# Depthwise convolution of a two-layer decoder step: four channel blocks on VectorE, four on TensorE between the pointwise blocks

## The reference

```python
def conv_module(x, prev, g_norm, w_pw1, b_pw1, w_dw, b_dw, g_ln, b_ln, w_pw2, b_pw2):
    h = rms_norm(x, g_norm)
    u = h @ w_pw1 + b_pw1
    a, gt = jnp.split(u, 2, axis=-1)
    u = a * jax.nn.sigmoid(gt)
    full = jnp.concatenate([prev, u], axis=1)
    c = lax.conv_general_dilated(full, w_dw[:, None, :], window_strides=(1,), padding='VALID',
                                 dimension_numbers=('NWC', 'WIO', 'NWC'),
                                 feature_group_count=CONV_CH) + b_dw
    c = jax.nn.silu(layer_norm(c, g_ln, b_ln))
    return x + c @ w_pw2 + b_pw2, full[:, -(CONV_W - 1):]
```

## Time and profile before

| | us |
|---|---|
| median of 3 runs | 1651.44 (1649.75 to 1652.22) |
| the profiled execution | 1650.97, its span 1648.9 |
| TensorE matmul busy | 1539.7 (93% of the span) |
| VectorE busy | 1276.7 (77%) |
| ScalarE busy | 960.0 (58%) |
| GpSimd busy | 159.9 (10%) |
| the stretch of the convolution stage, from the first pointwise block to the last mean matmul | 20 to 161 |

### The profile page before, as it was taken

One profiled execution on the slowest core, in us unless ns is written; L12 is line 12 of the kernel. 1 busy time (PEld: TensorE's weight loads), 2 busy tenths in 40 slices (PEclk: granted clock), 3 DMA queues, 4 the chain that ended last, 5 costly groups with the idle time before them and its releaser, 6 DMA issues.

```text
span 1648.9 us, 22208 instructions
## 1 busy us (share of the span) xinstructions
PE 1539.7 (93%) x7880; PEld 1291.9 (78%) x7880; DVE 1276.7 (77%) x1285; ACT 960.0 (58%) x999; POOL 159.9 (10%) x135
## 2 busy tenths in 40 slices
PE   6776899999988879999999999999999999999998
PEld 5765799999966768877877887887887887887886
DVE  5999545455686447888888888888888888888886
ACT  5420544344554246676667677677667677667674
POOL 5661111011230010000000000000000000000000
PEclk9888899999987979999999999999999999999999
DMA  8731234544533138988898898998998998998992
GB/s 329 141 115 31 77 136 158 176 158 166 180 97 143 52 124 305 350 347 339 348 369 325 338 373 324 350 356 328 353 360 322 338 365 329 358 356 331 345 359 115
DMA packets 64322, 431.38 MB, mean 262 GB/s; under 512 B 7862, under 2 KB 10166, under 8 KB 13713
## 3 DMA queue, kind: packets, MB, share of 16 engines
q1 hardware_dynamic: 57312, 412.38, 66.0%
q0 software_dynamic: 3616, 12.28, 3.2%
q10 hardware_dynamic: 3344, 6.05, 1.1%
HBM read 422.55 MB, written 9.14 MB: 262 GB/s over the span
## 4 chain that ended last, share of the span: by engine, by line
PE 77%; DVE 13%; issue 4%; ACT 3%; DMA 1%; POOL 1%; ACTq 0%; DVEq 0%; POOLq 0%
PE bank L334 23%; PE bank L336 23%; PE bank L335 23%; DVE odd L1175 2%; DVE C L1175 2%; PE bank L720 2%; DVE w_lo L1120 2%; ACT w_hi L1014 2%; DVE w_lo L1396 1%; PE bank L356 1%; PE bank L590 1%; PE bank L702 1%; PE bank L703 1%; DVE oe_lo L1538 1%; DVE d_lo L1493 1%
## 5 line engine op out<-in xcount | busy, mean ns | idle before, releaser
L1396 DVE TENSOR_TENSOR w_lo<-land,w_hi 128x2048 fp32r<-128x2048 f32 x224 | 504.1, 2289 | 109.9 <-ACT w_hi L1014 108.9
L1014 ACT CAST w_hi<-land 128x2048 fp32r<-128x2048 f32 x224 | 417.4, 1910 | 3.5 <-issue 3.5
L334 PE MATMUL bank<-w_hi,xe_hi 128*128 128x512 f32 x896 | 365.8, 408 | 0.6 <-DVE xe_lo L1482 0.6
L335 PE MATMUL bank<-w_lo,xe_hi 128*128 128x512 f32 x896 | 355.3, 397 | 0.0
L336 PE MATMUL bank<-w_hi,xe_lo 128*128 128x512 f32 x896 | 354.8, 396 | 0.0
L1017 ACT CAST d_hi<-land 128x2048 fp32r<-128x2048 f32 x112 | 214.1, 1912 | 125.3 <-PE bank L336 125.3
L1493 DVE TENSOR_TENSOR d_lo<-land,d_hi 128x2048 fp32r<-128x2048 f32 x112 | 256.7, 2292 | 23.9 <-ACT d_hi L1017 16.0
L336 PEld LDWEIGHTS bank<-w_hi,xe_lo 128*128 128x128 f32 x896 | 168.8, 188 | 41.0
L334 PEld LDWEIGHTS bank<-w_hi,xe_hi 128*128 128x128 f32 x896 | 168.8, 188 | 34.9 <-issue 1.0
L335 PEld LDWEIGHTS bank<-w_lo,xe_hi 128*128 128x128 f32 x896 | 169.3, 189 | 33.2
L334 PE MATMUL bank<-d_hi,heT_hi 128*128 128x512 f32 x448 | 178.4, 398 | 5.5 <-DVE heT_lo L1515 5.5
(11 more groups left out here) (244 smaller groups left out, 2289.4 us busy)
## 6 DMA issues: line engine op xcount, KB each, us to landing
land<-in_w_expert SPq DMA_DIRECT2D x336, 1024.0 KB, 5.1
land<-in_w_dense SPq DMA_DIRECT2D x54, 1024.0 KB, 4.8
rel_rows<-rb POOLq DMA_DIRECT2D x1, 3072.0 KB, 37.9
bias<-rel_rows ACTq DMA_DIRECT2D x4, 512.0 KB, 5.9
X<-in_x SPq DMA_DIRECT2D x4, 288.0 KB, 5.9
out_y<-X SPq DMA_DIRECT2D x2, 576.0 KB, 2.8
Us<-in_state POOLq DMA_DIRECT2D x1, 1088.0 KB, 9.5
out_conv_s<-Us POOLq DMA_DIRECT2D x1, 1088.0 KB, 6.5
```

What stands on the lines that cost most here:

```text
L334: pe.matmul(out, w[0], x[0], start=start, stop=False)
L335: pe.matmul(out, w[0], x[1], start=False, stop=False)
L1014: act.copy(w_hi[n % RING][:], land[(DENSE + u) % LAND][:]).then_inc(hi_done, 1)
L1396: dve.tensor_tensor(w_lo[n % RING][:], land[slot][:], w_hi[n % RING][:].bitcast(F32), ALU.subtract).then_inc(split, 1)
```

## The change

VectorE takes the prompt convolution of channel blocks 0, 2, 4 and 6, TensorE that of 1, 3, 5 and 7. TensorE runs the first three of its four directly behind pointwise blocks 3, 5 and 7, the fourth behind the third. ScalarE writes the diagonals, one 128x128 activation for each tap (identity, scaled by the tap's weight), the next channel block's as TensorE leaves each group. ScalarE no longer scales taps. VectorE also makes the window products of the sample convolution. Its taps behind the pointwise blocks are now 9, 3, 3, 33, 3, 33 and 3. GpSimd has no arithmetic left between the first low parts of the activations and those of the second matrix; it only issues its DMAs, the rows of the relative bias as soon as they are there, the two states when all of `Up` is.

```diff
-PE_CONV = 3
-POOL_CONV = 1
-DVE_CONV = KT_D - PE_CONV
-TAPS_BETWEEN = 6
+DVE_CHANNELS = [0, 2, 4, 6]
+PE_CHANNELS = [1, 3, 5, 7]
+CONV_BEHIND = {3: 0, 5: 1, 7: 2}
+TAPS_BEHIND = [9, 3, 3, 33, 3, 33, 3]
...
+            def conv(m):
+                if m == 0:
+                    pe.wait_ge(rb_ready, 1)
+                if m >= 2:
+                    pe.wait_ge(cp_ready, m - 1)
+                pe.wait_ge(u_ready, PE_CHANNELS[m] + 1)
+                for g, taps in enumerate(GROUPS):
+                    pe.wait_ge(diag_ready, CW * m + taps[-1] + 1)
+                    for w in taps:
+                        last = pe.matmul(bank[4 + m % 2][:, 0:SEQ], diag[:, g, w - taps[0], :],
+                                         Up[:, PE_CHANNELS[m], w:w + SEQ], start=(w == 0), stop=(w == CW - 1))
+                    last.then_inc(diag_used, 1)
+                pe.wait_ge(diag_used, len(GROUPS) * (m + 1))
+                pe.sem_inc(cv_done, 1)
...
+                if j in CONV_BEHIND:
+                    conv(CONV_BEHIND[j])
+            conv(3)
...
-            by_end = [*range(DVE_CONV - 1), *range(DVE_CONV, KT_D), DVE_CONV - 1]
+            by_end = [0, 2, 1, 3, 4, 5, 6, 7]
...
+            def diagonals(m, g):
+
+                if m >= 1:
+                    act.wait_ge(diag_used, len(GROUPS) * (m - 1) + g + 1)
+                for w in GROUPS[g]:
+                    act.activation(diag[:, g, w - GROUPS[g][0], :], ident, ACT.Identity,
+                                   scale=w_dw[:, PE_CHANNELS[m], w:w + 1]).then_inc(diag_ready, 1)
+
+            def conv_out(m):
+
+                act.wait_ge(cv_done, m + 1)
+                act.activation(C[:, PE_CHANNELS[m], 0:SEQ], bank[4 + m % 2][:, 0:SEQ], ACT.Identity,
+                               bias=v("b_dw", PE_CHANNELS[m])).then_inc(cp_ready, 1)
...
-                for w in range(4 * j, min(4 * j + 4, CW)):
-                    tap(w)
+                if j < 2:
+                    diagonals(0, 2 * j)
+                    diagonals(0, 2 * j + 1)
+                if j in CONV_BEHIND:
+                    for g in range(len(GROUPS)):
+                        diagonals(CONV_BEHIND[j] + 1, g)
+                    conv_out(CONV_BEHIND[j])
...
-                dve.wait_ge(win_ready, j + 1)
+                first = Us[:, j, :, 0:1]
+                windows = bass.AP(tensor=first.tensor, offset=first.offset,
+                                  ap=[list(first.ap[0]), [DS + CW - 1, NB], [1, DS], [1, CW]])
+                dve.wait_ge(u_ready, j + 1)
+                seq(dve.tensor_tensor(win[:], windows, w_dw[:, j, :].unsqueeze(1).unsqueeze(1).to_broadcast(
+                    [P, NB, DS, CW]), ALU.mult))
...
-            taps = [(j, w) for j in range(POOL_CONV, DVE_CONV) for w in range(CW)]
+            taps = [(j, w) for j in DVE_CHANNELS for w in range(CW)]
...
-                if j >= POOL_CONV:
-                    for t in taps[TAPS_BETWEEN * (j - 1):TAPS_BETWEEN * j]:
+                if j < KT_D - 1:
+                    for t in taps[sum(TAPS_BEHIND[:j]):sum(TAPS_BEHIND[:j + 1])]:
                         tap(*t)
             sample_conv(KT_D - 1)
-            for t in taps[TAPS_BETWEEN * (KT_D - 1):]:
+            for t in taps[sum(TAPS_BEHIND):]:
                 tap(*t)
...
-            def diagonals(m):
...
-            def add_tap(w):
...
+            pool.wait_ge(rb_ready, 1)
+            per_head = P * RLEN
+            pool.dma_start(bass.AP(tensor=io["rel_rows"].tensor, offset=0,
+                                   ap=[[per_head, NH], [RLEN, P], [1, RLEN]]),
+                           rb[:].unsqueeze(1).to_broadcast([NH, P, RLEN])).then_inc(rb_stored, 16)
+            pool.wait_ge(u_ready, KT_D)
             pool.dma_start(io["conv_p"], Up[:, :, SEQ:SEQ + CW - 1]).then_inc(conv_stored, 16)
             pool.dma_start(io["conv_s"], Us[:]).then_inc(conv_stored, 16)
```

More of the change, by code:

```diff
@@ L133, in build @@
         g_q8 = sb("g_q8", [P, 1])
-        prod = raw[:, :, 0:SEQ]
         phases = [0]
@@ L214, in build @@
         diag_ready, diag_used, cv_done, cp_ready = (sem(n) for n in ("diag_ready", "diag_used", "cv_done", "cp_ready"))
[L215 to L218, removed]
+        in_dw, cs_ready = (sem(n) for n in ("in_dw", "cs_ready"))
+        c_ready, mean_ready, xc_ready, ln_ready = (
+            sem(n) for n in ("c_ready", "mean_ready", "xc_ready", "ln_ready"))
         pw2_done, x_conv = sem("pw2_done"), sem("x_conv")
@@ L377, in _ @@
                     pe.matmul(bank[5][0:NH, 0:RLEN], relb[:, :], buckets[:, :], start=True, stop=True).then_inc(rel_sum, 1)
[L380 to L393, removed]
+                if j in CONV_BEHIND:
+                    conv(CONV_BEHIND[j])
+            conv(3)
             pe.wait_ge(cs_ready, KT_D)
-            by_end = [*range(DVE_CONV - 1), *range(DVE_CONV, KT_D), DVE_CONV - 1]
+            by_end = [0, 2, 1, 3, 4, 5, 6, 7]
             for k in by_end:
[L398 to L401, removed]
+                if k in DVE_CHANNELS:
+                    pe.wait_ge(c_ready, DVE_CHANNELS.index(k) + 1)
                 else:
-                    pe.wait_ge(cp_ready, k - DVE_CONV + 1)
+                    pe.wait_ge(cp_ready, PE_CHANNELS.index(k) + 1)
                 last = pe.matmul(MEAN[:, 0:T], c("mean_d"), C[:, k, :], start=(k == by_end[0]), stop=(k == by_end[-1]))
@@ L833, in _ @@
                                bias=v("b_g", j)).then_inc(sig_ready, 1)
-                for w in range(4 * j, min(4 * j + 4, CW)):
-                    tap(w)
-            hi_to(U_PW2 + RING)
[L837 to L842, removed]
+                if j < 2:
[5 more added lines that the diff above has]
+                    conv_out(CONV_BEHIND[j])
+            hi_to(U_PW2 + RING)
+            conv_out(3)
             for k in range(KT_D):
@@ L1169, in tap @@
                 elif w == 1:
-                    if j > POOL_CONV:
-                        dve.wait_ge(c_ready, j - POOL_CONV)
+                    if j > 0:
+                        dve.wait_ge(c_ready, DVE_CHANNELS.index(j))
                     ins = dve.tensor_scalar(acc, x, w_dw[:, j, w:w + 1], None, ALU.mult)
@@ L1209, in _ @@
                     sample_conv(j - 1)
-                if j >= POOL_CONV:
-                    for t in taps[TAPS_BETWEEN * (j - 1):TAPS_BETWEEN * j]:
+                if j < KT_D - 1:
+                    for t in taps[sum(TAPS_BEHIND[:j]):sum(TAPS_BEHIND[:j + 1])]:
                         tap(*t)
             sample_conv(KT_D - 1)
-            for t in taps[TAPS_BETWEEN * (KT_D - 1):]:
+            for t in taps[sum(TAPS_BEHIND):]:
                 tap(*t)
             dve.wait_ge(mean_ready, 1)
-            dve.wait_ge(c_ready, DVE_CONV - POOL_CONV)
-            dve.wait_ge(cg_ready, POOL_CONV)
+            dve.wait_ge(c_ready, len(DVE_CHANNELS))
             dve.wait_ge(cs_ready, KT_D)
-            dve.wait_ge(cp_ready, PE_CONV)
+            dve.wait_ge(cp_ready, len(PE_CHANNELS))
             for k in range(KT_D):
@@ L1574, in _ @@
             h_lo_even(0, range(0, KT_D, 2), H_hi, H_lo)
-            pool.wait_ge(in_con, 16)
-            pool.wait_ge(in_dw, 16)
-            diagonals(0)
-            def add_tap(w):
[L1581 to L1607, removed]
+            pool.wait_ge(rb_ready, 1)
[4 more added lines that the diff above has]
+            pool.wait_ge(u_ready, KT_D)
             pool.dma_start(io["conv_p"], Up[:, :, SEQ:SEQ + CW - 1]).then_inc(conv_stored, 16)
```

## The result

The changed kernel takes 1622.18 us (median of 4 runs, 1621.87 to 1622.62), beside 1650.62 us for the kernel before (4 runs); the ratio is 0.983, with a 95% interval of 0.9815 to 0.984. The forecast was 1623.9. The profiled execution took 1621.87, its span 1620.1, which is 28.8 us less than the span of before.

The account below looks back on a forecast made before the run. VectorE, slowed by GpSimd, was taken to bound the convolution stage. Moving the mean from 161.34 to 136.0 saves 25.3 us, plus 2.2 for the squares, 27.5 in all: 1623.9 us, 8 in 10 range 1619 to 1634.

Parts of the forecast that it names:

- Which engine ends the stage: Convolution stage: TensorE's blocks sum to 131.3 us, then eight mean matmuls take 4.4, so VectorE subtracts the mean at 136.0.
- The bare mean passes: End of the convolution stage: 14 mean matmul passes formerly hidden under the taps now lie bare, costing 3.9 us.
- The slack: VectorE in the convolution stage: ends at 125, TensorE asks for its last block at 134.6, 9.6 us of slack.
- Splits freed: VectorE: splits 1 to 3 no longer stretch to 10.76 us beside GpSimd's diagonals; it comes free at 33.1, not 37.0.
- the other estimate, 36 us for 124: ScalarE's 124 diagonals priced by the Trainium skill's fixed and per-column costs; the sum was the same either way.
- The squares: Second normalisation after the stage: TensorE at full clock, six distances of 0.36 us less, 2.2 us saved.
- The other reading: Squares after the stage: short idles between matmul groups can throttle TensorE's clock again, losing only the 2.2 us.
- The reason given for the doubled tap: VectorE's taps: GpSimd's work beside them, not busy TensorE or DMA, doubles a tap from 0.40 to 0.88 us.
- the rival on the slower side: Convolution taps: 0.88 us is the price beside busy TensorE and DMA, VectorE ends at 185, kernel 1674; chance 0.03.

## Why the prediction was right

- **Which engine ends the stage.** Forecast: TensorE, 16 mean passes queued behind its fourth block. So it was. Its sum was to reach 131.3 and reached 130.7, since a pointwise block takes about 6.43 and not 6.52 (three of them fill 30.21 to 49.50). The mean passes were to take 4.4 and took 4.12: eight took 2.21 and sixteen take 4.12, so each further one costs 0.24. The forecast's 0.276 had a start and an end in it, about 0.3 us, that come once for a row and not for each pass. The mean was to be subtracted at 136.0 and was at 134.88. This 1.1 us is most of the miss of 1.7.
- **The bare mean passes.** They are the one new cost, 3.9 us in the sum, and they are there.
- **VectorE.** Forecast to end at 125, ended at 125.7; the product at 1.15, measured 1.17, and 1.22 with what follows it; the tap at 0.40. The slack was to be 9.6 and was 7.8, since TensorE asked sooner and VectorE ended 0.7 later.
- **Splits freed.** From 10.76 to 6.70 us for three, VectorE free at 33.1, as forecast.
- **ScalarE.** 0.30 for a diagonal, as scaled down from the wider tap; the other estimate, 36 us for 124, comes to 0.29 each and fits too. It cost nothing on the path.
- **The squares.** Forecast 2.2 us less at full clock. From the mean to the reciprocal it went from 9.19 (170.53 - 161.34) to 7.30, so 1.9; the squares go 0.67 apart and not 0.60. The other reading, that short gaps between matmuls would lose the full clock, did not come true: it is 1.00 from 135 to 141, with TensorE busy 4.81 of the 6 us.
- **The reason given for the doubled tap** was argued from timing rows only. The run in which GpSimd adds for nobody shows it, and also that the rival on the slower side had the right mechanism with the wrong owner: at 0.88 a tap VectorE does become the end, by 16.8 us for 67 us of GpSimd work.
- **What lay outside the sum.** At the reciprocal the changed kernel is 28.35 us ahead (170.53 - 142.18), at the end of the span 28.8, where 27.5 was forecast. The attention stretch told of above begins at 492.85 before and at 464.88 now, 28.0 ahead, and ends at 554.28 and 525.05, 29.2 ahead. Had that stretch taken the 61.4 us of before and all else been equal, the gain would have been 27.6, an estimate. So about 1.2 us of the gain rest on something that the prediction did not have and no run explains; the range was wide enough for either. The rest of the miss, 0.5, is the distance from span to median, 2.5 before and 2.1 now.

The change looks like an interleaving of TensorE's blocks, and the prediction priced it as sums of work alone, without saying why the place should be worth nothing. The run with all blocks behind shows that the interleaving is indeed without a price of its own.

## What to carry to other kernels

Two engines that share a resource must be priced together: before moving an operation to a third, idle engine, look at what the first one's instructions last beside it, and compare the stall with the operation's own time on the first engine (here 1.9 us of stall against 1.22 us). Sum each engine's work over the stage in its new order, and take the longest; the difference to the second longest is the slack that says how much more may be moved (here 7.8 us, and seven taps moved into it won 3.5). And work that was hidden under the old bound comes out bare under the new one, so look for it behind the last instruction of the engine that now ends the stage.

## What the runs showed of the hardware that I had not expected

- GpSimd and VectorE stretched each other, one operation at a time. Beside GpSimd's additions a tap went from 0.40 to 0.88, a split of 2048 columns from 2.28 to 2.83 and a multiplication of a single tile from 0.41 to 0.82. The additions took 0.72 beside a reduction, 1.58 beside a window product and 2.66 beside a split, 1.05 in the mean (66.94 / 64). The window product, which had started first, kept its 1.18.
- TensorE kept its full clock through 5.28 us of squares in which it worked by pairs with gaps (4.81 us busy in the 6 us from 135 to 141), when it came out of dense work. After 6.6 us of idling the same squares ran at half clock to near their end and took 7.40.
- Extra matmuls held the clock at 1.00 over 6 us of idle time and were worth 1.0 us at the place, which the median of five runs did not show.
